# Expert rows of a decoder trunk by slot: tables in DRAM instead of select matmuls, and stationary router weights

## The reference

```python
def moe_swiglu(h, w_router, w1, w3, w2):
    logits = h @ w_router                        # 256 x 8
    top_v, top_i = lax.top_k(logits, 2)
    top_w = jax.nn.softmax(top_v, axis=-1)
    gate = sum(one_hot(top_i, 8) * top_w[..., None], axis=-2)
    for e in range(8):                           # w1, w3: 1024 x 3584, w2: 3584 x 1024
        y = y + gate[..., e:e+1] * ((silu(h @ w1[e]) * (h @ w3[e])) @ w2[e])
    return y                                     # x = x + y
```

## Time and profile before

| | us |
|---|---|
| median of 3 runs | 1592.51 (1592.32 to 1595.32) |
| profiled execution | 1593.62 |
| its span, first to last instruction | 1591.8 |
| PE busy | 1549.4 (97%) |
| DVE busy | 1267.9 (80%) |
| ACT busy | 1052.8 (66%) |
| DMA | 445.34 MB, mean 280 GB/s |

### The profile page before, as it was taken

The page is one execution under the profiler, slowest core; times in us unless marked ns, Lnnn a source line. Parts: engine busy times, 40 slices in busy tenths (PEclk is TensorE's granted clock), DMA queues, the critical chain, the costliest instruction groups (busy, mean ns, idle before and its releaser), DMA issues.

```text
span 1591.8 us, 23204 instructions
## 1 busy us (share of the span) xinstructions
PE 1549.4 (97%) x7253; PEld 1271.5 (80%) x7253; DVE 1267.9 (80%) x1329; ACT 1052.8 (66%) x1159; POOL 5.9 (0%) x12
## 2 busy tenths in 40 slices
PE   7999999999999899999999999999999999999997
PEld 6888888788888778878878878877887887887885
DVE  5885655446976679789789789789889979978978
ACT  6565544336564467677687687687778768767766
POOL 0000000000000000000000000000000000000000
PEclk9999999999999789999999999999999999999999
DMA  9444565358543679799899999999989989989985
GB/s 331 159 159 133 185 198 167 107 191 282 167 160 109 233 228 302 255 369 371 288 375 370 312 354 367 338 329 371 374 296 370 370 297 367 369 293 372 372 305 193
DMA packets 361372, 445.34 MB, mean 280 GB/s; under 512 B 17728, under 2 KB 272744, under 8 KB 361336
## 3 DMA queue, kind: packets, MB, share of 16 engines
q1 hardware_dynamic: 360768, 442.73, 82.1%
q0 software_dynamic: 480, 2.13, 0.4%
q10 hardware_dynamic: 88, 0.02, 0.0%
HBM read 443.76 MB, written 1.05 MB: 279 GB/s over the span
## 4 chain that ended last, share of the span: by engine, by line
PE 83%; DMA 4%; issue 4%; DVE 4%; ACT 3%; SPq 1%; DVEq 0%; ACTq 0%
PE bank L748 25%; PE bank L750 25%; PE bank L749 25%; DMA w_raw<-in_moe_w 4%; PE bank L1036 2%; ACT w_hi L450 2%; PE bank L1062 2%; DVE w_lo L1127 1%; SPq L351 1%; DVE hT_lo L1517 1%; PE bank L830 1%; PE bank L774 1%; ACT hT_hi L739 0%; DMA x_residual<-in_x 0%; PE bank L814 0%
## 5 line engine op out<-in xcount | busy, mean ns | idle before, releaser
L1127 DVE TENSOR_TENSOR w_lo<-w_raw,w_hi 128x1024 fp32r<-128x1024 f32 (+1 forms) x448 | 780.9, 1755 | 113.9 <-ACT w_hi L450 113.1
L450 ACT ACTIVATE w_hi<-w_raw 128x1024 fp32r<-128x1024 f32 (+1 forms) x448 | 663.9, 1492 | 160.2 <-PE bank L750 145.2
L748 PE MATMUL bank<-w_hi,hT_hi 128*128 128x512 f32 (+1 forms) x1424 | 568.4, 399 | 6.6 <-DVE hT_lo L1517 2.5
L750 PE MATMUL bank<-w_hi,hT_lo 128*128 128x512 f32 (+1 forms) x1424 | 555.6, 390 | 0.0
L749 PE MATMUL bank<-w_lo,hT_hi 128*128 128x512 f32 (+1 forms) x1424 | 554.4, 389 | 0.0
L748 PEld LDWEIGHTS bank<-w_hi,hT_hi 128*128 128x128 f32 x1424 | 269.3, 189 | 63.6 <-issue 6.7
L750 PEld LDWEIGHTS bank<-w_hi,hT_lo 128*128 128x128 f32 x1424 | 269.0, 189 | 56.7
L749 PEld LDWEIGHTS bank<-w_lo,hT_hi 128*128 128x128 f32 x1424 | 269.9, 190 | 50.8
L1122 DVE TENSOR_TENSOR w_lo<-w_raw,w_hi 128x2048 fp32r<-128x2048 f32 (+2 forms) x100 | 201.5, 2019 | 96.8 <-ACT w_hi L444 96.0
L444 ACT ACTIVATE w_hi<-w_raw 128x2048 fp32r<-128x2048 f32 (+2 forms) x100 | 169.6, 1699 | 161.1 <-PE bank L750 159.7
L748 PE MATMUL bank<-w_hi,hiddenM_hi 128*128 128x512 f32 x448 | 178.8, 399 | 1.1
(11 more groups left out here) (230 smaller groups left out, 1022.2 us busy)
## 6 DMA issues: line engine op xcount, KB each, us to landing
w_raw<-in_moe_w SPq DMA_DIRECT2D x448, 512.0 KB, 8.0
w_raw<-in_moe_w SPq DMA_DIRECT2D x448, 256.0 KB, 4.9
w_raw<-in_w_in SPq DMA_DIRECT2D x64, 512.0 KB, 4.6
w_raw<-in_dense_w SPq DMA_DIRECT2D x44, 512.0 KB, 4.8
w_raw<-in_dense_w SPq DMA_DIRECT2D x44, 256.0 KB, 2.8
w_raw<-in_w_out SPq DMA_DIRECT2D x16, 512.0 KB, 4.6
w_raw<-in_w_pool_proj SPq DMA_DIRECT2D x8, 512.0 KB, 4.5
w_raw<-in_w_attn_proj SPq DMA_DIRECT2D x8, 512.0 KB, 4.1
```

Source lines behind the costliest of these rows:

```text
L450: act.activation(whi[:, m % SLOTS, 0:n], raw8[m % 8][:, 0:n], ACT.Copy).then_inc(s_hi, 1)
L748: pe.matmul(dst, ahi, bhi, start=start, stop=False)
L750: return pe.matmul(dst, alo, bhi, start=False, stop=stop)
L1127: dve.tensor_tensor(wlo[:, m % SLOTS, 0:n], raw8[m % 8][:, 0:n], whi[:, m % SLOTS, 0:n], ALU.subtract).then_inc(s_lo, 1)
```

## The change

- **In DRAM** there are two tables with 128 rows for each of 12 jobs: `x_by_slot` and `y_by_slot`. POOL clears them after its last load of pool weights (16 DMAs, 512-byte pieces).
- **x rows.** After `gather(0)`, which stays a product (reordered: all of the first 128 tokens, then all of the rest), ACT makes normed x (`xn`, two copies of 128x1024), POOL scatters it with four indirect DMAs (two choices by two halves of the tokens). SP loads the 128 rows of the next job in every job (`xg`, 0.5 MB), ahead of the first down chunk's load. `gather(i + 1)` is now 8 transposes.
- **ACT waits** for the four scatters in block 1 of each job; SP waits for them before the `xg` load.
- **y rows.** The y copies go to `ysb`, SP stores it (0.5 MB) after the loads of the next job's chunks 0 to 7. After the last job SP waits for the store, POOL gathers with four indirect DMAs, and DVE adds four times (128x1024) with the gate of each choice.
- **Gone** in the loop: `scatter`, `selT`, the matmuls for it, `selR` beyond the first, `ylo`, `add_rows`; and the gates by job.
- **Router.** The 8 router columns are stationary and 256 tokens move: 24 matmuls into a transposed result, which DVE copies and PE transposes back (two small transposes). The norm on DVE stands behind that copy. ACT loads the square root's table earlier. `keep_busy` adds 4, 9, 3 and 6 matmuls of 512 columns without use of their result.

```diff
                 group(up_chunk, i, e, 24, 6)
+                sp.wait_ge(s_xsc, 2 * TT * 16)
+                sp.wait_ge(s_g, i * 2 + 2)
+                sp.dma_start(xg[:], xslot[bass.ds(i * P + P, P), :]).then_inc(s_xg, 16)
                 group(down_chunk, i, e, 28, 0)
+            def store_y(i):
+                sp.wait_ge(m_y, i * 2 + (LEAD + 2))
+                sp.dma_start(yslot[bass.ds(i * P, P), :], ysb[:]).then_inc(s_ys, 16)
             def next_job(i, e):
                 for g in range(2):
                     group(up_chunk, i, e, JOB_CHUNKS + 4 * g, g)
+                store_y(i)
...
+            store_y(njobs - 1)
+            sp.wait_ge(s_ys, njobs * 16 + 16)
+            sp.nop().then_inc(s_go, 1)
...
+            pool.memset(zt[:], 0.0).then_inc(s_z0, 1)
+            for j in range(NJ):
+                pool.dma_start(xslot[P * j:P * j + P, :].rearrange("p (o n) -> p o n", n=128), zeros).then_inc(s_xz, 16)
+            for j in range(E, NJ):
+                pool.dma_start(yslot[P * j:P * j + P, :].rearrange("p (o n) -> p o n", n=128), zeros).then_inc(s_xz, 16)
+            pool.wait_ge(s_xz, (2 * NJ - E) * 16)
+            pool.wait_ge(s_row, 1)
+            for c in range(2):
+                for t in range(TT):
+                    if c == 0:
+                        pool.wait_ge(s_xn, t + 1)
+                    pool.indirect_dma_start(xslot, bass.IndirectOffsetOnAxis(rowu[:, c * TT + t:c * TT + t + 1], 0),
+                                            xn[:, t, :], None).then_inc(s_xsc, 16)
+            pool.wait_ge(s_go, 1)
+            for t in range(TT):
+                for c in range(2):
+                    pool.indirect_dma_start(yg[c][t], None, yslot,
+                                            bass.IndirectOffsetOnAxis(rowu[:, c * TT + t:c * TT + t + 1], 0)
+                                            ).then_inc(s_yg[c * TT + t], 16)
...
             gathered_hi(0)
+            for t in range(TT):
+                act.activation(xn[:, t, :], X[:, t, :], ACT.Copy, scale=st[:, 3, t:t + 1]).then_inc(s_xn, 1)
...
                         if first and u == 1:
-                            act.wait_ge(s_st, i + 1)
-                            act.activation(selT[:], bank[1][:, 0:S], ACT.Copy).then_inc(s_sts, 1)
+                            act.wait_ge(s_xsc, 2 * TT * 16)
...
-                    for t in range(TT):
-                        ins = three(bank[4 + t][:, 0:E], hThi[:, k, t * P:t * P + P], hTlo[:, k, t * P:t * P + P],
-                                    wrhi[:, k, :], wrlo[:, k, :], k == 0, k == KC - 1)
+                    ins = three(bank[4][0:E, 0:S], wrhi[:, k, :], wrlo[:, k, :], hThi[:, k, :], hTlo[:, k, :],
+                                k == 0, k == KC - 1)
...
+                pe.wait_ge(s_xg, i * 16)
                 for j in range(2):
                     for q in range(4):
                         k = 4 * j + q
-                        for t in range(TT):
-                            for x in (xrhi, xrlo):
-                                ins = pe.matmul(bank[2 + j][:, q * P:q * P + P], x[:, t, k * P:k * P + P],
-                                                selR[:, t, :], start=(t == 0 and x is xrhi),
-                                                stop=(t == TT - 1 and x is xrlo))
+                        ins = pe.transpose(bank[2 + j][:, q * P:q * P + P], xg[:, k * P:k * P + P], ident)
...
                         chunk(c, [bank[4 + u][:]], hehi, helo, 0, 512, True, False, i * jd + it, tiles=1)
-                        if first and u == 1:
-                            scatter(i)
```

More of the change, by code:

```diff
@@ L604, in layer @@
                     ahead(c + 25)
+                else:
+                    act.activation(sq0[:], cst[:, C_ONE:C_ONE + 1], ACT.Sqrt)
                 hT_hi(3 * l + 2, 16 + 8 * l, (2, 3))
@@ L1007, in _, with keep_busy @@
                 down_d(k, (1,))
+            def keep_busy(n, b):
+                for _ in range(n):
+                    pe.matmul(bank[b][:], aThi[:, 0, 0:P], aThi[:, 0:2, :], start=True, stop=True)
             layer(1, LAYER1, first=lambda: x_T(2, 1))
+            keep_busy(4, 5)
             x_T(3, 1)
@@ L1026, in _ @@
             pe.matmul(bank[7][:, 0:E], ones, tmp8[:, 1, :], start=False, stop=True).then_inc(s_pos, 1)
+            keep_busy(3, 0)
             def gather(i):
-                pe.wait_ge(s_sel, i + 1)
+                if isinstance(i, int):
+                    pe.wait_ge(s_sel, 1)
+                    for t in range(TT):
+                        pe.wait_ge(s_xrl, t + 1)
+                        for j in range(2):
+                            for q in range(4):
+                                k = 4 * j + q
+                                for x in (xrhi, xrlo):
+                                    ins = pe.matmul(bank[2 + j][:, q * P:q * P + P], x[:, t, k * P:k * P + P],
+                                                    selR[:, t, :], start=(t == 0 and q == 0 and x is xrhi),
+                                                    stop=(t == TT - 1 and x is xrlo), skip_group_check=True)
+                            if t == TT - 1:
+                                ins.then_inc(s_g, 1)
+                    return
+                pe.wait_ge(s_xg, i * 16)
                 for j in range(2):
@@ L1033, in gather @@
                         k = 4 * j + q
-                        for t in range(TT):
-                            for x in (xrhi, xrlo):
-                                ins = pe.matmul(bank[2 + j][:, q * P:q * P + P], x[:, t, k * P:k * P + P],
-                                                selR[:, t, :], start=(t == 0 and x is xrhi),
-                                                stop=(t == TT - 1 and x is xrlo))
-                    ins.then_inc(s_g, 1)
[L1041 to L1051, removed]
+                        ins = pe.transpose(bank[2 + j][:, q * P:q * P + P], xg[:, k * P:k * P + P], ident)
+                    ins.then_inc(s_g, 1)
             gather(0)
-            pe.wait_ge(s_y0, 1)
+            keep_busy(6, 0)
             pe.wait_ge(s_tab, 1)
@@ L1077, in pair @@
                             hiddenT_m(b - 1, 1 - u)
-                        if first and u == 1:
-                            for t in range(TT):
-                                ins = pe.matmul(bank[1][:, t * P:t * P + P], selR[:, t, :], identR[:],
-                                                start=True, stop=True)
-                            ins.then_inc(s_st, 1)
                         chunk(c + 1, [bank[4 + u][:]], hehi, helo, 4, 512, False, True, i * jd + it, tiles=1)
@@ L1088, in _ @@
                     pair(it)
-                pe.wait_ge(m_xa, i * 4 + 4)
                 gather(i + 1)
@@ L1104, in _ @@
                     ins.then_inc(s_use, 1)
-            scatter(njobs)
         @block.vector
@@ L1351, in layer @@
                 hT_lo(3 * l + 2, 16 + 8 * l, (2, 3))
-                norm(2 * l + 1)
-            for s in (s_flo, m_flo, m_ylo):
+                if l == 0:
+                    norm(1)
+            for s in (s_flo, m_flo):
                 dve.nop().then_inc(s, LEAD)
@@ L1447, in _, with rows_lo @@
             dve.nop().then_inc(s_mk, 1)
-            for t in range(TT):
+            def rows_lo(t):
                 dve.wait_ge(s_xr, t + 1)
```

140 lines of the change are left out of this document (73 added, 67 removed).

## The result

The changed kernel takes 1618.22 us (median of 4, 1614.76 to 1619.31) where the kernel before, on the same chip, takes 1592.41 (1591.96 to 1595.32). The ratio is 1.0154, 95% interval 1.0135 to 1.0174. The profiled execution took 1619.31 us with a span of 1617.5. The forecast was 1566.0, with a range from 1555 to 1582, and slower had a chance of 4%.

The account below looks back on a forecast made before the run. The prediction took PE (busy 97%) to bound the loop, with DMA leading at job changes. Its terms, -9.5 - 20.0 - 2.2 + 0 - 1.7 + 2.8 + 0 + 4, sum to -26.6 us, giving 1565.9 us, range 1555 to 1582.

Parts of the forecast that it names:

- rival B: Loop: transfers take over, the two new ones falling in full on the path; +16 us, 1582 us; chance 18%.
- Clearing the tables: Mixer, from 373 us: 8.4 MB cleared while nobody waits for a weight DMA; 0 us, bounds 0 and 2.
- y store: Up part of later jobs: 0.52 MB delays chunks 8 and later by 1.4 us, some 0.4 a job; +2.8 us.
- Scatter in the seven later jobs: Job changes: the removed 2.0 us only filled a wait, so PE waits longer; 0 us, bounds 0 and -14.
- The gathers: Between up and down part: eight gathers become 8 transposes each, 2.5 us less apiece with full gain; -20.0 us.
- Routing: Up to the loop: earlier logits and a faster gather start the loop's first matmul 6.8 us earlier; -9.5 with later matmuls.
- D: Routing: keep_busy does not hold PE's clock; the sum is 6 us less, 1572 us; chance 13%.
- first 13 matmuls: Start of the loop: they take 2.9 us instead of 5.7 with the clock held, another 2.7 us gained.
- ACT's wait for the scatters: Job 0, block 1: scatters land at 562, before PE needs the result at 568.5; 0 us, bounds 0 and 4.
- The end: After the last down matmul: store, four indirect gathers and additions take about 17.3 us for 13.6; +4, bounds +1 and +15.
- C: Scatters and end: indirect DMAs slow on POOL, eating the gain from 6.2 us each; 1607 us at 8; chance 4%.
- A: Job changes: the queue moves up and the scatter's time is gained in full or half; 1552 to 1559 us; chance 13%.

Follow-up runs that it names:

- a_align: Changed kernel plus 224 unused bytes a partition, so raw weight slots 4 to 7 start at multiples of 256 bytes again: 1588.9 us.
- b_shift32: Kernel before plus one unused 4-byte tile (32 bytes padded), moving slots 4 to 7 to 32 past a multiple of 256 bytes: 1621.2 us.
- c_y_twice: Changed kernel with slots 4 to 7 aligned and early clears, y stored a second time per job into an unread DRAM table: 1584.4 us.
- b_all256: Kernel before with two paddings, so all eight raw weight buffers start at multiples of 256 bytes: 1580.2 us.
- c_fill: Changed kernel with slots 4 to 7 aligned and early clears, plus eight unread matmuls per job where the scatter stood: 1575.3 us.
- best1: Changed kernel with all eight slots aligned, early clears and eight unread fill matmuls per job: 1562.6 us.
- c_no_keep: Changed kernel with slots 4 to 7 aligned and early clears, without the four keep_busy calls (22 matmuls fewer): 1580.9 us.
- a_align_clears: Changed kernel with slots 4 to 7 aligned, table clears moved to layer 0's dense part, one 0.5 MB block at a time: 1581.4 us.
- c_all256: Changed kernel with all eight slots aligned and early clears, without fill matmuls: 1563.4 us.

## Why the prediction was wrong

**The step that failed: DMA's rate was taken as a property of the kernel.** The prediction held 368 GB/s for both kernels and rival B reckoned with it too. It was the mean of 348 and 385, and how much of the time has which rate hangs on addresses that the change moved without naming them: the diff adds three tiles ahead of the buffers. Of a job's 45.1 MB some 29.9 move in the up part and 15.2 in the down part; at 348 and 386 GB/s they need 85.9 + 39.4 = 125.3 us, more than the 124.6 that the prediction left for the whole period. With DMA's idle time at the step to the down part (2.3 us in the period from 909.8, the DMA share summed over windows of 1 us) that is 127.6 of the 129.6 measured; no row places the last 2 us. The step is worth +29.3 us (1618.2 to 1588.9, shown by a_align and, from the other side, b_shift32). B's mechanism, transfers taking over, is what happened; its reason, more bytes, was not. With no slot aligned the kernel before moves 1.1 MB a job less and has the longer period (130.9 for 129.6), and one more store of y costs 2.9 us (c_y_twice). That PE's 97% made it the bound was the same mistake seen from PE (b_all256). In the earlier trace rows the two windows were 24 us wide, one period of the eight slots; windows of 4 us would have shown two rates at one DMA share.

The forecast missed by 52.3 us. Three edits, one after the other, take back 29.3 (addresses), 7.5 (clears) and 6.2 (clock); the 9 us left between c_fill and the forecast lie in the smaller terms below.

**Clearing the tables: 0 expected, 7.5 to 10.9 measured**, 10.4 by the mark at `add_out`, outside the bounds of 0 and 2. "Nobody waits for a weight DMA" in the mixer was true of loads that have the engines for themselves. 8.4 MB take 21 us at the 394 GB/s of that stretch, and a load issued meanwhile shares the engines with them. The prediction gave such a bound for the y store and none here. The Trainium skill (DMA: Bandwidth & Descriptors, SWDGE vs HWDGE vs iDMA) says that an engine takes turns between the queues that POOL and SP feed; the landing of 13.9 us for 4.6 agrees.

**Scatter in the seven later jobs: 0 for its time was right, the sign was not.** PE waits 3.3 to 3.6 us where 3 to 3.5 was said. The step stopped there: a longer wait at an unchanged end was taken to cost nothing. Behind it PE runs at 1.2 GHz for some 5 us, and 0.9 us a job of that reaches the time (125.9 to 125.0 in c_fill).

**The gathers**: eight transposes take 1.03 us, as expected. Their 2.5 us with `selT`'s 0.25, less 0.4 for the store, make 2.3 a job. At four aligned slots the period falls by 1.4 and, with the fill that holds the clock, by 2.1 (127.1 to 125.0 in c_fill); at eight by 2.0, and by 2.4 with the fill (best1). The term was right where PE leads, and at 348 GB/s it buys 1.3.

**Routing**: -4.6 up to the loop's first matmul for -6.8. The read of the logits moved by 2.75 us as worked out; `keep_busy` held the clock through the router and not through the gather, so neither the forecast nor D was right, but a time between. It was close: in a_align, with the same instructions, the clock held through the gather too, and the stretch shrank by 8.6 us. The 2.7 us for the first 13 matmuls is not there: c_no_keep has them slow and ends no later, because ACT's wait for the scatters comes next.

**ACT's wait for the scatters: 0 expected, 4.4 us of ACT and 1.7 of PE measured**. The forecast's cost was time of PE, and 1.7 is within its bounds of 0 and 4. The kernel after, POOL and ACT:

```profile
567.30 2.32 POOL L465 DMA_INDIRECT x_by_slot<-x_scaled_rows,row_of_choice  x1 [154.71 <-ACT x_scaled_rows L735]
...
572.49 2.93 POOL L465 DMA_INDIRECT x_by_slot<-x_scaled_rows,row_of_choice  x1 [0.30 <-issue]
...
581.73 0.38 ACT L748 ACTIVATE hiddenM<-bank 128x256 f32<-128x256 f32 x1 [4.38 <-DMA x_by_slot<-x_scaled_rows,row_of_choice]
```

The scatters start after `xn`, which stands behind the gather's evacuation on ACT, and not when the row numbers are ready.

**The end: +6.8 for +4.** It is 20.4 us for 13.6:

```profile
1598.41 1.06 ACT L790 ACTIVATE y_slot_rows<-bank 128x512 f32<-128x512 f32 x2
1599.66 0.35 SPq L401 DMA_DIRECT2D y_by_slot<-y_slot_rows  x1
1602.62 2.07 POOL L470 DMA_INDIRECT y_first_choice<-y_by_slot,row_of_choice  x1 [1027.20 <-SPq L436]
...
1607.51 0.94 POOL L470 DMA_INDIRECT x_scaled_rows<-y_by_slot,row_of_choice  x1 [0.30 <-issue]
1607.99 1.28 DVE L1616 SCALAR_TENSOR_TENSOR x_residual<-y_first_choice,gate_probs,x_residual 128x1024 f32<-128x1024 f32 x1 [4.14 <-DMA y_first_choice<-y_by_slot,row_of_choice]
1610.47 1.28 DVE L1616 SCALAR_TENSOR_TENSOR x_residual<-x_scaled_rows,gate_probs,x_residual 128x1024 f32<-128x1024 f32 x1 [1.20 <-DMA x_scaled_rows<-y_by_slot,row_of_choice]
...
1613.13 1.28 DVE L1616 SCALAR_TENSOR_TENSOR x_residual<-x_scaled_rows,gate_probs,x_residual 128x1024 f32<-128x1024 f32 x1
```

The copies and the store are nearly as worked out (+5.5 for +5.1). The first two gathers let DVE go on 5.4 and 5.5 us after their issue, and the last three additions of 1.28 us stand in a row. The last gather is issued at 1607.51, so at 5.4 us it lands at 1612.9, just ahead of the last addition at 1613.13: both chains, issues and additions, end together. The chain that I had summed was the right one, and its gathers were sized too small: three issues and a landing take 4.9 + 5.4 us and not the 7.8 set down.

**Rivals.** C is excluded: an indirect DMA takes 0.94 to 2.9 us on POOL, and 6.2 for each would have been needed. What A had in mind is seen in part once the DMA is faster: one and the same wait of PE is 3.53 us in a_align_clears and 2.28 in c_all256. The rival on the slower side should have been B, with a rate and not a volume as its price. The 358 GB/s that the Trainium skill gives as a core's bound (DMA: Bandwidth & Descriptors, Where 436 GB/s comes from) do not bound this kernel: with aligned buffers 385 and 406 GB/s are held.

## What to carry to other kernels

When a diff allocates anything ahead of a DMA's destination, look up where that buffer starts before and after, and put it at a multiple of 256 bytes on purpose. Where the profile shows two plateaus of GB/s at one full DMA share, suspect this first. A mean rate is no property of a kernel, a busy share of 97% is no proof of a bound, and a bulk transfer that nobody waits for is still paid by the loads it shares the engines with. Work that fills a wait may be what keeps PE's clock up: when it is taken out, ask what the longer idle time does to the clock.

## What the hardware showed unexpectedly

- A destination off a multiple of 256 bytes costs 4.2 to 4.5 ns for each piece of a transfer: 348 for 385 GB/s with 1 KB pieces, 386 for 406 with 2 KB. In kernels whose PE is busy 97% of the time that is 13 to 41 us of 1600 (1580.2, 1593.1, 1621.2 for the same instructions).
- Sixteen 0.5 MB stores of zeros in 512-byte pieces, issued by POOL at once, tripled the landing time of loads issued by SP; issued one by one in another stretch they landed in 5.2 us each and cost nothing that shows (layer 1's last `add_out` at 533.5 us, for 534.6 in the kernel before).
- Behind PE waits of 3.3 to 3.6 us the granted clock fell to 0.50 seven times of seven (after), behind 3.0 to 3.5 five of seven (a_align_clears), behind 2.2 to 2.8 once of six (c_all256), behind 1.6 or less never; but once behind 1.79 (b_shift32).
- PE's busy time is no measure of its work alone: the same 7253 matmuls were busy for 1536.9, 1549.4 and 1567.4 us as the weights came later, each time 97% of the span.
